# Applying each expert's gates on eviction and combining with rounded products in a two-layer decoder trunk

## The reference, cut to what matters

```python
logits = xt @ router                       # 256 x 8
topv, topi = lax.top_k(logits, 2)
gates = jax.nn.softmax(topv, axis=-1)
yb = swiglu(xblk, wg[e], wu[e], wd[e])     # expert e on the rows routed to it
y = yb * row_gate[:, None]                 # each row by its gate
out = zeros(t, d).at[row_tok].add(y)       # back to the tokens, summed
x = x + out
```

## Time and profile before

| what | value |
|---|---|
| time, median of 3 runs | 1745.4 us (1743.64 to 1746.65) |
| the profiled execution's own time | 1745.86 us |
| its span, first to last instruction | 1744.1 us |
| TensorE busy | 1681.1 us, 96% of the span |
| VectorE busy | 1254.0 us, 72% |
| ScalarE busy | 1030.2 us, 59% |
| granted TensorE clock, mean | 0.977 of full speed |
| HBM read | 434.37 MB, 250 GB/s over the span |

### The profile page before, as it was taken

The page is one execution under the profiler, slowest core; times in us unless marked ns, Lnnn a source line. Parts: engine busy times, 40 slices in busy tenths (PEclk is TensorE's granted clock), DMA queues, the critical chain, the costliest instruction groups (busy, mean ns, idle before and its releaser), DMA issues.

```text
span 1744.1 us, 28714 instructions
## 1 busy us (share of the span) xinstructions
PE 1681.1 (96%) x11060; PEld 1445.8 (83%) x11060; DVE 1254.0 (72%) x1423; ACT 1030.2 (59%) x1236; POOL 36.3 (2%) x40
## 2 busy tenths in 40 slices
PE   7999889999999998799999999999999999999997
PEld 6888789999988887788888888888888888788785
DVE  1455545455414654489899899899899898998996
ACT  2334144444423241388788788788787787787784
POOL 0003000000000030000000000000000000000000
PEclk9999889999989998799999999999999999999999
DMA  6402155555414201489999899899899899999993
GB/s 211 169 26 75 41 201 175 189 183 180 158 48 145 97 3 50 144 326 378 351 346 374 315 373 378 314 372 376 314 376 372 315 375 359 333 372 343 348 377 133
DMA packets 189925, 436.65 MB, mean 250 GB/s; under 512 B 8832, under 2 KB 11408, under 8 KB 189712
## 3 DMA queue, kind: packets, MB, share of 16 engines
q1 hardware_dynamic: 187040, 433.49, 69.2%
q10 hardware_dynamic: 2800, 1.96, 0.4%
HBM read 434.37 MB, written 1.05 MB: 250 GB/s over the span
## 4 chain that ended last, share of the span: by engine, by line
PE 61%; DVE 1%; issue 0%; ACT 0%; DVEq 0%; ACTq 0%
PE bank L640 18%; PE bank L642 18%; PE bank L641 17%; PE bank L623 4%; PE bank L736 2%; PE bank L1130 1%; PE bank L1073 0%; DVE w_lo L1730 0%; PE bank L648 0%; DVE arena L1928 0%; ACT w_hi L1202 0%; DVE arena L1561 0%; ACT arena L1202 0%; PE bank L957 0%; DVE arena L1834 0%
## 5 line engine op out<-in xcount | busy, mean ns | idle before, releaser
L1202 ACT ACTIVATE w_hi<-ring 128x1024 fp32r<-128x1024 f32 x772 | 815.8, 1061 | 321.0 <-PE bank L642 320.8
L1730 DVE TENSOR_TENSOR w_lo<-ring,w_hi 128x1024 fp32r<-128x1024 f32 x672 | 814.7, 1223 | 76.5 <-ACT w_hi L1202 26.4
L640 PE MATMUL bank<-w_hi,acts_hi 128*128 128x512 f32 x1344 | 531.1, 395 | 2.8 <-DVE acts_lo L1938 1.4
L642 PE MATMUL bank<-w_hi,acts_lo 128*128 128x512 f32 x1344 | 523.8, 390 | 0.0
L641 PE MATMUL bank<-w_lo,acts_hi 128*128 128x512 f32 x1344 | 523.1, 389 | 0.0
L640 PEld LDWEIGHTS bank<-w_hi,acts_hi 128*128 128x128 f32 x1344 | 252.4, 188 | 55.1 <-issue 1.7
L642 PEld LDWEIGHTS bank<-w_hi,acts_lo 128*128 128x128 f32 x1344 | 252.2, 188 | 53.0
L641 PEld LDWEIGHTS bank<-w_lo,acts_hi 128*128 128x128 f32 x1344 | 252.5, 188 | 52.2 <-issue 1.7
L1721 DVE TENSOR_TENSOR w_lo<-ring,w_hi 128x1024 fp32r<-128x1024 f32 x84 | 102.6, 1225 | 117.0 <-ACT w_hi L1202 116.9
L640 PE MATMUL bank<-acts_hi,w_hi 128*128 128x256 f32 x608 | 174.8, 288 | 1.6 <-DVE acts_lo L1529 1.6
L641 PE MATMUL bank<-acts_lo,w_hi 128*128 128x256 f32 x608 | 173.6, 286 | 0.0
(11 more groups left out here) (185 smaller groups left out, 1240.7 us busy)
## 6 DMA issues: line engine op xcount, KB each, us to landing
ring<-in_moe_wg SPq DMA_DIRECT2D x112, 1024.0 KB, 5.2
ring<-in_moe_wu SPq DMA_DIRECT2D x112, 1024.0 KB, 5.4
ring<-in_moe_wd SPq DMA_DIRECT2D x112, 1024.0 KB, 4.9
ring<-in_w_in SPq DMA_DIRECT2D x24, 1024.0 KB, 6.5
ring<-in_dense_wg SPq DMA_DIRECT2D x14, 1024.0 KB, 5.1
ring<-in_dense_wu SPq DMA_DIRECT2D x14, 1024.0 KB, 5.1
ring<-in_dense_wd SPq DMA_DIRECT2D x14, 1024.0 KB, 4.8
ring<-in_w_o SPq DMA_DIRECT2D x8, 1024.0 KB, 7.4
```

The source lines that it names most:

```text
L640: pe.matmul(out_, a_hi, b_hi, start=first, stop=False, **kw)
L642: return pe.matmul(out_, a_lo, b_hi, start=False, stop=final, **kw)
L1202: return act.activation(o, i, ACT.Copy, **kw)
L1730: TT(w_lo[:, q, :], raw, w_hi[:, q, :].bitcast(F32), ALU.subtract).then_inc(lo_ready, 1)
```

## The change

The gate is applied when the output leaves PSUM, and the scatter is done with two rounded products in place of a float32 one.

- ScalarE writes the two halves of `yg_hi` = round(gate x output) by an Identity activation with a per-partition scale `gate_e`, in place of two copies. It waits for `cbe_ready` first.
- VectorE has a new function, `low_output`: for each half one scalar_tensor_tensor, output x gate - `yg_hi`, into `yg_lo`. It stands between split g0 and split u0 of the next expert. For the last expert it stands before `add`.
- `gate_e` is the row sum of `combine[:, e, :]` and `combine_e` is that matrix compared with zero (a bare 0/1 matrix, fp32r). Both are made by VectorE behind `multiply(6)` of the same expert; the copy at the top of the expert is gone.
- TensorE's scatter waits for `yg_low` and does, for each of the four outputs, a product with `yg_hi` and one with `yg_lo`.
- `yg_hi`, `yg_lo` lie in the second halves of acts_hi and acts_lo, `combine_e` in da_lo. The first turn of an expert waits for `cb_kept` in place of `cbe_ready`; VectorE's wait for `cb_kept` ahead of the loop moves to the new instructions.

```diff
--- before.py
+++ after.py
@@ -222,7 +222,7 @@
         onehot = moe.take(2 * NE * P).rearrange("p (b e s) -> p b e s", b=2, e=NE)
         gated = moe.take(2 * NE * P).rearrange("p (b e s) -> p b e s", b=2, e=NE)
         combine = moe.take(NE * T).rearrange("p (e t) -> p e t", e=NE)
-        combine_e = moe.take(T)
+        gate_e = moe.take(1)
         act_b = [moe.take(CW) for _ in range(2)]
         sil_b = [moe.take(CW) for _ in range(2)]
 
@@ -232,8 +232,8 @@
         assert dense.at <= 22 * T + 2 * RW
         mask_in = sq_qk.rearrange("p k t -> p (k t)")[:, 0:12 * C]
 
-        gated_all = gated.rearrange("p b e s -> p (b e s)")
-        yg = gated_all[:, D:2 * D]
+        combine_e = da_lo[:, 0:T]
+        yg_hi, yg_lo = acts_hi[:, KT * P:KT * T], acts_lo[:, KT * P:KT * T]
 
         def da_parts(j):
 
@@ -393,6 +393,7 @@
         route_act = sem("route_act")
         route_exp = sem("route_exp")
         flag_ready = sem("flag_ready")
+        yg_low = sem("yg_low")
         oh_ready = sem("oh_ready")
         gated_ready = sem("gated_ready")
         cb_done = sem("cb_done")
@@ -1125,7 +1126,7 @@
                     if j:
                         pe.wait_ge(at_low, at1 * NJ + j)
                     else:
-                        pe.wait_ge(cbe_ready, at1 + 1)
+                        pe.wait_ge(cb_kept, 4 * p + 4)
                     for i in range(4):
                         last_ = pe.transpose(bank[6][:, i * P:(i + 1) * P], act_b[j % 2][:, i * P:(i + 1) * P],
                                              ident)
@@ -1143,12 +1144,13 @@
 
                 def scatter(at1):
 
-                    pe.wait_ge(yg_kept, at1 * 2 + 2)
+                    pe.wait_ge(yg_low, at1 * 2 + 2)
                     pe.wait_ge(cbe_ready, at1 + 1)
                     for f in range(4):
                         b, hf = f // 2, f % 2
-                        mm(bank[(6, 7, 4, 5)[f]][:, :], combine_e[:, b * P:(b + 1) * P],
-                           yg[:, hf * 512:(hf + 1) * 512]).then_inc(sct_done, 1)
+                        cs, hs = slice(b * P, (b + 1) * P), slice(hf * 512, (hf + 1) * 512)
+                        mm(bank[(6, 7, 4, 5)[f]][:, :], combine_e[:, cs], yg_hi[:, hs], True, False)
+                        mm(bank[(6, 7, 4, 5)[f]][:, :], combine_e[:, cs], yg_lo[:, hs], False, True).then_inc(sct_done, 1)
 
                 def expert(e, at1, last_one):
 
@@ -1471,8 +1473,10 @@
                         split("g", 0, at1 + 1)
 
                     act.wait_ge(pc_free, at1 * PIECES_E + (2 * PIECES_E + PIECES))
+                    act.wait_ge(cbe_ready, at1 + 1)
                     for hf in range(2):
-                        copy(yg[:, hf * 512:(hf + 1) * 512], bank[4 + hf][:, :]).then_inc(yg_kept, 1)
+                        act.activation(yg_hi[:, hf * 512:(hf + 1) * 512], bank[4 + hf][:, :], ACT.Identity,
+                                       scale=gate_e).then_inc(yg_kept, 1)
                     if not last_one:
                         split("u", 0, at1 + 1)
                         silu(0, at1 + 1)
@@ -1951,6 +1955,13 @@
                     TT(at_lo[:, j % 2, :], bank[6][:, :], at_hi[:, j % 2, :].bitcast(F32), ALU.subtract).then_inc(
                         at_low, 1)
 
+                def low_output(at1):
+                    for hf in range(2):
+                        hs = slice(hf * 512, (hf + 1) * 512)
+                        dve.wait_ge(yg_kept, at1 * 2 + (hf + 1))
+                        STT(yg_lo[:, hs], bank[4 + hf][:, :], gate_e, yg_hi[:, hs].bitcast(F32), ALU.mult,
+                            ALU.subtract).then_inc(yg_low, 1)
+
                 def add(at1):
 
                     for f in range(4):
@@ -1960,7 +1971,6 @@
                         TT(o, o, bank[(6, 7, 4, 5)[f]][:, :], ALU.add).then_inc(sct_added, 1)
 
                 def expert(e, at1, last_one):
-                    dve.tensor_copy(combine_e, combine[:, e, :]).then_inc(cbe_ready, 1)
                     split("g", 1, at1)
                     multiply(0, at1)
                     split("u", 1, at1)
@@ -1973,12 +1983,17 @@
                         turned(j - 1, at1)
                         split("d", j - 1, at1)
                     multiply(NJ - 1, at1)
+                    dve.wait_ge(cb_kept, 4 * p + 4)
+                    dve.tensor_reduce(gate_e, combine[:, e, :], AX.X, ALU.add)
+                    TS(combine_e, combine[:, e, :], 0.0, None, ALU.is_gt).then_inc(cbe_ready, 1)
                     split("d", NJ - 1, at1, range(0, TURN_AT))
                     turned(NJ - 1, at1)
                     split("d", NJ - 1, at1, range(TURN_AT, 4))
                     if not last_one:
                         gathered(at1 + 1)
                         split("g", 0, at1 + 1)
+                    low_output(at1)
+                    if not last_one:
                         split("u", 0, at1 + 1)
                     add(at1)
                     dve.wait_ge(sct_added, at1 * 4 + 4)
@@ -1988,7 +2003,6 @@
                 if p:
                     split("g", 0, first)
                 split("u", 0, first)
-                dve.wait_ge(cb_kept, 4 * p + 4)
                 dve.wait_ge(act_turned, 8)
                 with dve.Fori(0, NE - 1) as e:
                     expert(e, e + first, False)
```

## The result

| | median | range | runs |
|---|---|---|---|
| before | 1744.52 us | 1742.80 to 1746.65 | 4 |
| changed | 1731.72 us | 1730.06 to 1732.90 | 4 |

Two later timings of the same changed kernel, against fresh runs of the one before, gave 0.9933 (0.9919 to 0.9947) and 0.9937 (0.9921 to 0.9953); the forecast was 1734.6 / 1745.4 = 0.9938, which lies inside all three intervals. The profiled execution took 1731.21 us, with a span of 1729.4.

What follows compares the result with a forecast made beforehand. TensorE was taken to bound the loop, with VectorE and the transfers near rivals. Seven passes of 1.62 - 0.1 us plus 0.2 us in the last expert gave 10.8 us off 1745.4, so 1734.6 us, range 1732 to 1740.

Steps and rivals of the forecast that it cites:

- The bound and TensorE's term: Expert loop is bound by TensorE; the scatter goes from 3.44 to 1.82 us, saving 1.62 us in each of 8 experts.
- VectorE's chain and the slack: From split g0 to split g1, subtractions delay the first g1 remainder: 1.6 us slack spent, 0.1 us stall per expert.
- ScalarE, the row sum, the comparison: Activations 0.6 to 0.7 us each, hidden at the transition; row sum and comparison 0.6 us, covered ahead of split d.
- The table loads: Rival: Silu and Identity switching in the loop loads tables twice per expert, 1.28 us each; total 1741.5 us, chance 0.06.
- The transfers: Rival: DMA transfers need the scatter's pause to catch up, pass stays at 124.56 us; total 1745 us, chance 0.04.
- The tail: Serial end of the last expert, from ScalarE's output to the last add: gain 0.2 us, between -0.3 and +0.4.
- The range: Total time from 1732 us (no stall, less run spread) to 1740 us (a stall of 0.8 us).

## Why the prediction was right, and where it was wrong

**The bound and TensorE's term: right.** 3.44 us became 1.82. The products twice give that price by itself, and the moved gates with the old product show that nothing else contributes.

**VectorE's chain and the slack: right.** The prediction said that the change spends the 1.6 us of slack at the first piece of g1 to within 0.1 us. The subtractions came at 0.744 us (the prediction had 0.74, where its own rate gives 0.475 + 0.256 = 0.73), the first remainder at 867.88 + 1.2 where TensorE wanted it at 869.20, and the stall is 0.05 to 0.07 us, where 0.1 was taken. That it is spent is shown from both sides: 1.32 us more on VectorE cost 1.32 us, 0.91 us less on TensorE gave nothing.

**ScalarE, the row sum, the comparison: right.** The activations are 674 ns (0.6 to 0.7), 90 ns above the copies of the same shape into acts_hi (584). The Trainium skill, "ScalarE: Activation LUTs", section "What ACT_TABLE_LOAD costs", has 93 ns for an operand by pointer, and this trace agrees. The gates have cover where they stand and cost 0.62 us where they have none.

**The table loads: none,** as the row of L1323 had it. The Trainium skill, "ScalarE: Activation LUTs", section "Table sets: the hidden batching unit", has identity in every set, and this trace agrees: no load stands in the loop, where Silu and Identity alternate. **The transfers:** the share rose to 0.98 and no engine waited for one, in passes as short as 122.35 us too.

**The tail: right in sign.** 0.14 us in place of 0.2. The first add comes 0.77 us behind the scatter's start (0.75 in the prediction), and each next one 0.6 us after; the scatter itself starts 1.04 us later within the tail, where 0.95 was forecast.

**The range: wrong, and this is the step that failed:** "1745.4 - 11.6 with no stall is 1733.8, less 1.8 for the spread of the runs, 1732". The size of the change was well inside (10.8 forecast, 10.9 between the parts behind the gather), but the 1.8 us was read from three runs of the kernel before, which spanned 3.0 us. Runs of that kernel afterwards go from 1740.90 to 1750.36 us, and both medians enter the difference. Of the 2.9 us between 1734.6 and 1731.72, 0.9 is the kernel before, whose median was 1744.52 in this timing where the forecast started from 1745.4, and 2.0 the larger difference. The first timing of the changed kernel, 1731.72, is the lowest of three (1734.20 and 1733.58 followed). In the profiles, what moves them lies ahead of the loop: up to 4.9 us, where the same 40 matmuls were granted 0.74 of full clock in one execution and 0.86 in another. The profile of before alone had its hint in the clock, 0.977 for the whole span beside 1.00 in the loop: the part ahead of the loop is not at full clock, so it need not be the same each time. I did not turn that into a term. The mean clock of the whole span tells no more than that: it was 0.977 and 0.976 in two profiles of one kernel that were 5.0 us apart. Why the clock is granted differently from execution to execution stays open; nothing here tried it.

## What to carry to other kernels

Work out when the next product is wanted and when its operand is ready, in the transition of the loop, before and after: the gain of a shorter product is the smaller of what it saves and that slack, here 1.6 us, nearly all. Once it is spent the two engines are tied: more on VectorE costs in full, less on TensorE gives nothing, and the next gain must take from both. For the range, look at how much of the program runs below full clock, profile the same kernel twice to see how far that part moves, and allow for its spread in both medians; to size a change of 1% in a loop, the pass of the loop in the profile (0.01 us from run to run here) tells more than the total.

## What had not been expected of the hardware

The total of one program varied by 5.0 us between two profiles with all of it, to 0.1 us, ahead of the first gather (1014.8 and 1014.7 us behind it). Between an add and the next VectorE instruction, a wait for its own adds cost 0.61 us, where instructions with no such wait start 0.1 us before the former ends.
